# Seven products for eight in half of the blocks of the second MLP's down projection

## The chip, the core and the metric

The kernel runs on one core of a Trainium2 chip. The metric is device time in microseconds. Five engines work beside each other, each through a queue of its own in order: TensorE (PE; its weight loads are listed as PEld), VectorE (DVE), ScalarE (ACT), GpSimd (POOL) and SyncE (SP), which issues most of the DMAs. They are ordered among each other by semaphores that the program writes out by hand: a waiting instruction holds up everything behind it on its engine.

## What is computed

Two layers over 256 frames of 2048 channels, in float32. Each layer ends in an MLP, and the second layer's is what matters here:

```python
D_MODEL = 2048; SEQ = 256; D_FF = 4 * D_MODEL
...
        h = rmsnorm(x, ffn_norm[layer])
        x = x + jnp.square(jax.nn.relu(h @ w_up[layer])) @ w_down[layer]
```

`w_up` is 2048 x 8192 and `w_down` 8192 x 2048. The hidden layer is worked through in four quarters of 2048.

## The kernel before

**Precision by splitting.** Every weight is split into a high part (ScalarE's rounding copy, `Wh`, L1160) and the rest (VectorE's subtraction, `Wl`, L1585); the left operand likewise, into the halves of `A1` and `A2`. A product is high x high + high x low + low x high, three matmuls in the down projection.

**Weights.** They come in units of 512 KB, 1024 columns per partition, through four buffers `raw`, `Wh`, `Wl`. SyncE loads a unit into a raw buffer when VectorE has done the low split of the unit that was in it (`lo_split`). ScalarE splits it when it has landed and TensorE has finished the unit that held the buffer before (`unit_done`); VectorE follows (`hi_split`), TensorE waits for `lo_split`.

**Up projection.** Per quarter eight blocks of 256 hidden channels (`pair`, L710), four units each. The block's result lies in two PSUM banks of `ps`; blocks alternate between two pairs of banks. When it is done, ScalarE copies the crossed terms out (L1165), VectorE adds them to the rest (L1659, counted in `pair_read`), multiplies by the norm (L1918), squares the positive part (L1920, `hid_ready`), and ScalarE (L1539) and VectorE (L1923) split the result into `A2`. On both engines these steps stand behind the four splits of the next block's units.

**Down projection.** Per quarter four column blocks of 512 (`token_block`, L671). A unit is 256 hidden rows x 512 columns: for both halves of the 256 frames and both of its hidden chunks of 128, three matmuls with 512 columns, 12 in all (L681 to L683). A column block's two banks are accumulated over 8 units; then VectorE adds them to `xin` (`block_read`, L1680) while the next block accumulates in the other two banks. The bank set `px` is not used in this stage, and GpSimd has no work in the second MLP.

**Loops.** SyncE, ScalarE and VectorE run the quarters as loops (`load_mlp`, `double_pairs`, `downs`); TensorE's program is written out.

Of the kernel before, what the change touches and what calls it, by code (L numbers as in the profile page):

```python
# [32 lines left out]
P = 128  # L33
# [103 lines left out]
def trunk_kernel(nc, x, mix_norm_e, w_in_e, conv_w, conv_b, lru_wa, lru_ba, lru_wx, lru_bx, lru_lambda,  # L137
# [4 lines left out]
    with ctx:  # L142
# [46 lines left out]
        with ExitStack() as o:  # L189
            lt = sb("lt", [P, LC, L], on=o)  # L190
# [162 lines left out]
        zeroed = sem("zeroed")  # L353
        block = ctx.enter_context(nc.Block())
# [117 lines left out]
        def block_banks(g0, b):  # L472

            return 2 * ((g0 + b) % 2)

# [19 lines left out]
        def _(sp):  # L495
# [128 lines left out]
            load_mlp(P_MLP1, 1, blocks=True)  # L624
# [3 lines left out]
            for b in range(3):  # L628
                sp.wait_ge(pair_read, g + 2 * (b + 1))
                sp.dma_start(frames[:, :, bass.ts(b, 512)], xin[:, :, bass.ts(b, 512)]).then_inc(out_stored, 16)  # L630
# [7 lines left out]
        def _(pe):  # L638
# [32 lines left out]
            def token_block(g, d, at, freed, by_halves=False, beside=None):  # L671

                pe.wait_ge(pair_read, freed)

                def products(u, h):
                    for c in range(2):
                        k = 2 * u + c
                        high = A2[:, k, h * P:h * P + P]
                        low = A2[:, k, L + h * P:L + h * P + P]
                        to = ps[:, d + h, :]  # L680
# [18 lines left out]
            def opening(form, b, A):  # L699
# [4 lines left out]
                for c, low in order:  # L704
                    if low:
                        mm(ps[:, b, 0:L], Wl[:, 0, c, 0:P], A[:, c, 0:L], start=False, stop=False)
                    else:
                        mm(ps[:, b, :], Wh[:, 0, c, 0:P], A[:, c, :], start=(c == 0), stop=False)

            def pair(g, d, A, ready=None, base=0, per_unit=0, turn=0, beside=None, freed=None, form=None):  # L710


                b = 2 * d
# [4 lines left out]
                for s in range(NU):  # L718
# [3 lines left out]
                    if form and s == 0:  # L722
                        opening(form, b, A)
                    for t in range(1 if form and s == 0 else 0, 2):
                        for c in range(UK):
# [3 lines left out]
                            mm(ps[:, b + t, :], Wh[:, s, c, cols], A[:, k, :], start=(n == 0), stop=False)  # L729
                            last = mm(ps[:, b + t, 0:L], Wl[:, s, c, cols], A[:, k, 0:L], start=False, stop=(n == KC - 1))  # L730
# [378 lines left out]
            def token_mlp(g0, a1_at, a1_unit, a2_at, norm):  # L1109
# [13 lines left out]

                for q in range(QTR):
                    for j in range(8):
                        g = q * 16 + j + g0
                        freed = g - 1
                        if j == 0:
                            freed = g - 2 if q else g0 - 4
                        if q == 0 and j == 1:  # L1130
                            freed = g0 - 4
                        pair(g, g % 2, A1, a1_ready, a1_at, a1_unit, freed=freed,
                             beside=last_block if q == 0 and j == 0 else None,
                             form=entry_form(q, j))
                    for b in range(4):
                        g = q * 16 + (g0 + 8 + 2 * b)
                        token_block(g, block_banks(g0, b), q * 8 + a2_at, g - 2 if b else g - 1,
                                    by_halves=q == QTR - 1 and b == 3)
# [5 lines left out]
        def _(act):  # L1144
# [387 lines left out]
            def token_mlp(g0):  # L1532

                def up(j, d, q=0):
                    first = isinstance(q, int) and q == 0 and isinstance(j, int) and j == 0
                    pair(q * 16 + j + g0, (g0 + d) % 2, beside=last_operand if first else None)
                    hid.wait(act)
                    c = (g0 + d) % 2
                    hi.inc(fn(A2[:, bass.ds(j * 2, 2), 0:L], cross[:, c], ACT.Copy))  # L1539

# [11 lines left out]
                def downs(q, n=8):  # L1552
                    for j in range(n):
                        for s in range(NU):
                            split(q * 16 + (g0 + 9 + j), s)

                double_pairs(act, 8, up, (hi, 2), (hid, 2), first=2)
                downs(0)
                with trips(act, QTR - 2, (hi, 8), (hid, 8)) as q:
                    double_pairs(act, 8, lambda j, d: up(j, d, q + 1), (hi, 2), (hid, 2))  # L1560
                    downs(q + 1)
                double_pairs(act, 8, lambda j, d: up(j, d, QTR - 1), (hi, 2), (hid, 2))
                downs(QTR - 1, 7)

# [4 lines left out]
        def _(dve):  # L1569
# [374 lines left out]
            def token_mlp(g0):  # L1944
# [10 lines left out]
                def token_up(j, d, q=0):  # L1955
                    first = isinstance(q, int) and q == 0 and isinstance(j, int) and j == 0
                    up(g0, j, d, q, False, after=q * 8 + j + (CROSSED1 + 1),
                       beside=last_operand if first else None)

                double_pairs(dve, 8, token_up, (hi, 2), (seq, 2), first=2)  # L1960
                downs(g0, 0)
                with trips(dve, QTR - 2, (hi, 8), (seq, 8)) as q:
                    double_pairs(dve, 8, lambda j, d: token_up(j, d, q + 1), (hi, 2), (seq, 2))
                    downs(g0, q + 1)
                double_pairs(dve, 8, lambda j, d: token_up(j, d, QTR - 1), (hi, 2), (seq, 2))
                downs(g0, QTR - 1, halved=2)
# [458 lines left out]


# [27 lines left out]
```

## Time and profile before

| | |
|---|---|
| median of 3 runs | 1984.74 us (1984.61 to 1985.82) |
| profiled execution, span from first to last instruction | 1982.2 us |
| TensorE busy | 1953.0 us, 99% |
| VectorE, ScalarE, GpSimd busy | 1251.1, 916.4, 648.3 us |
| mean granted clock of TensorE | 0.995 of full speed |

The profile is one execution, recorded instruction by instruction. It gives for each instruction its start, its duration and the idle time before it with what ended that. The second MLP runs from about 1276 us to the end. In the records a matmul of 512 columns lasts 0.39 us, but matmuls are pipelined and their ends are modelled: the distance between starts is what one costs. Durations of GpSimd instructions include time in which they stand.

### The profile page before, as it was taken

The page shows a single profiled execution, that of the slowest core. Times are in us where ns is not written, and L with a number is a line of the kernel's source. Part 1 is how long each engine was busy: PE and PEld are TensorE (multiplying, and loading weights), DVE is VectorE, ACT ScalarE, POOL GpSimd, SP SyncE. Part 2 cuts the span into 40 slices and gives each one's busy share as a digit, 9 for nine tenths or more (in the row PEclk, how much of TensorE's full clock was granted, in tenths as well). Part 3 has the DMA queues.
Part 4 walks back from the last instruction along what each step waited for, and adds up shares of the span by engine and source line. Part 5 has one row for each costly group of instructions (what it writes and reads, how often), then busy time and mean ns, then how long its engine had stood idle before and what let it go on. Part 6 is the DMA issues. An engine that isn't in the chain of part 4 may idle for free.

```text
span 1982.2 us, 31585 instructions
## 1 busy us (share of the span) xinstructions
PE 1953.0 (99%) x11578; PEld 1651.1 (83%) x11578; DVE 1251.1 (63%) x1378; ACT 916.4 (46%) x1222; POOL 648.3 (33%) x858
## 2 busy tenths in 40 slices
PE   8999999999999999999998999999999999999999
PEld 7888788888888888888877888888888888888887
DVE  6885768755765576566559655576556556655654
ACT  6467654443443444344453544544344434434443
POOL 3592439778687778440019300000000000000000
PEclk9999999999999999999998999999999999999999
DMA  7644576666666666686788666655665666566654
GB/s 226 181 134 144 175 197 194 204 231 210 206 210 224 211 204 232 206 268 193 251 281 303 183 183 199 184 181 192 193 192 188 195 195 188 190 196 183 197 194 162
DMA packets 285582, 400.19 MB, mean 202 GB/s; under 512 B 23328, under 2 KB 185264, under 8 KB 283408
## 3 DMA queue, kind: packets, MB, share of 16 engines
q1 hardware_dynamic: 278032, 371.77, 59.7%
q0 software_dynamic: 5216, 24.52, 4.0%
q8 instruction: 93, 1.52, 0.3%
q10 hardware_dynamic: 2208, 2.11, 0.3%
q14 instruction: 33, 0.27, 0.0%
HBM read 371.87 MB, written 25.17 MB: 200 GB/s over the span
## 4 chain that ended last, share of the span: by engine, by line
PE 92%; DVE 2%; ACT 2%; DMA 1%; POOL 1%; issue 1%; SPq 0%; ACTq 0%; DVEq 0%; POOLq 0%
PE ps L729 27%; PE ps L730 13%; PE ps L681 12%; PE ps L683 12%; PE ps L682 12%; PE px L1059 1%; PE px L1061 1%; PE px L1060 1%; PE ps L1059 1%; PE ps L1060 1%; PE ps L1061 1%; PE px L945 1%; DMA raw<-in_w_up_dram 1%; PE ps L666 1%; DVE Wl L1585 1%
## 5 line engine op out<-in xcount | busy, mean ns | idle before, releaser
L1585 DVE TENSOR_TENSOR Wl<-raw,Wh 128x1024 fp32r<-128x1024 f32 x660 | 843.6, 1288 | 616.9 <-ACT Wh L1160 614.6
L1160 ACT ACTIVATE Wh<-raw 128x1024 fp32r<-128x1024 f32 x660 | 691.8, 1059 | 750.7 <-PE ps L683 377.3
L729 PE MATMUL ps<-A,Wh 128*128 128x512 f32 x2364 | 830.1, 396 | 2.7 <-DVE A L1672 2.3
L730 PE MATMUL ps<-A,Wl 128*128 128x256 f32 x2364 | 657.6, 278 | 0.0
L729 PEld LDWEIGHTS ps<-A,Wh 128*128 128x128 f32 x2364 | 443.3, 188 | 108.7 <-issue 5.1
L730 PEld LDWEIGHTS ps<-A,Wl 128*128 128x128 f32 x2364 | 444.7, 188 | 0.3
L681 PE MATMUL ps<-Wh,A 128*128 128x512 f32 x1024 | 399.8, 390 | 0.0
L683 PE MATMUL ps<-Wh,A 128*128 128x512 f32 x1024 | 398.5, 389 | 0.0
L682 PE MATMUL ps<-Wl,A 128*128 128x512 f32 x1024 | 398.4, 389 | 0.0
L683 PEld LDWEIGHTS ps<-Wh,A 128*128 128x128 f32 x1024 | 192.2, 188 | 40.3
L681 PEld LDWEIGHTS ps<-Wh,A 128*128 128x128 f32 x1024 | 192.2, 188 | 39.9
L682 PEld LDWEIGHTS ps<-Wl,A 128*128 128x128 f32 x1024 | 192.2, 188 | 39.5
L1923 DVE TENSOR_TENSOR A<-cross,A 128x512 f32 (+1 forms) x64 | 47.1, 736 | 57.6 <-ACT A L1539 32.5
L1411 ACT ACTIVATE A<-cross 128x512 fp32r<-128x512 f32 (+1 forms) x32 | 20.3, 634 | 106.4 <-DVE cross L1920 106.4
L1539 ACT ACTIVATE A<-cross 128x512 f32 (+1 forms) x32 | 20.3, 634 | 95.8 <-DVE cross L1920 95.8
L1659 DVE TENSOR_TENSOR cross<-ps,cross 128x512 f32<-128x512 f32 x75 | 51.2, 683 | 7.7 <-ACT cross L1165 7.6
L2375 POOL DMA_DIRECT2D us<-s_u x8 | 7.2, 897 | 139.8 <-DMA s_u<-uc 139.8
L1059 PE MATMUL ps<-Wh,A 128*128 128x512 f32 x128 | 51.1, 399 | 1.0 <-DVE Wl L1585 1.0
L1680 DVE TENSOR_TENSOR xin<-ps,xin 128x512 f32<-128x512 f32 x68 | 43.8, 682 | 11.2 <-PE ps L683 11.2
L2325 POOL TENSOR_TENSOR t<-cti,lamp 128x256 f32<-128x256 f32 x16 | 21.6, 1352 | 89.0 <-ACT cti L1365 89.0
L1920 DVE SCALAR_TENSOR_TENSOR cross<-cross 128x512 f32<-128x512 f32 x64 | 48.6, 760 | 2.2
L1059 PE MATMUL px<-Wh,A 128*128 128x512 f32 x128 | 50.0, 390 | 0.0
(376 smaller groups left out, 2035.5 us busy)
## 6 DMA issues: line engine op xcount, KB each, us to landing
raw<-in_w_up_dram SPq DMA_DIRECT2D x256, 512.0 KB, 3.9
raw<-in_w_down_dram SPq DMA_DIRECT2D x256, 512.0 KB, 3.9
raw<-in_w_glu_dram SPq DMA_DIRECT2D x64, 512.0 KB, 4.4
raw<-in_w_in_e_dram SPq DMA_DIRECT2D x52, 512.0 KB, 3.9
raw<-in_w_out_e_dram SPq DMA_DIRECT2D x32, 512.0 KB, 3.8
s_params<-stg POOLq DMA_DIRECT2D x16, 1024.0 KB, 6.1
slot<-s_params SPq DMA_DIRECT2D x12, 768.0 KB, 7.3
slot<-s_params SPq DMA_DIRECT2D x12, 256.0 KB, 7.5
```

The lines of the kernel that those rows point to most:

```text
L681: mm(to, high, wide(Wh, u % NU)[:, c], start=(k == 0), stop=False)
L682: mm(to, high, wide(Wl, u % NU)[:, c], start=False, stop=False)
L683: last = mm(to, low, wide(Wh, u % NU)[:, c], start=False, stop=(k == KC - 1))
L729: mm(ps[:, b + t, :], Wh[:, s, c, cols], A[:, k, :], start=(n == 0), stop=False)
L730: last = mm(ps[:, b + t, 0:L], Wl[:, s, c, cols], A[:, k, 0:L], start=False, stop=(n == KC - 1))
L1059: mm(to, high, wide(Wh, u % NU)[:, c], start=(k == 0), stop=False)
L1160: fn(Wh[:, s], raw[:, s], ACT.Copy).then_inc(hi_split, 1)
L1585: tt(Wl[:, s], raw[:, s], Wh[:, s].bitcast(F32), ALU.subtract).then_inc(lo_split, 1)
L1659: tt(cross[:, d] if dest is None else dest, banks[:, :, 0:L], cross[:, d], ALU.add).then_inc(pair_read, 1)
L1680: tt(to, banks[:, h, :], to, ALU.add).then_inc(pair_read, 1)
L1920: stt(cross[:, c], cross[:, c], 0.0, cross[:, c], ALU.max, ALU.mult).then_inc(hid_ready, 1)
L1923: tt(A2[:, k, L:2 * L], cross[:, c], A2[:, k, 0:L].bitcast(F32), ALU.subtract).then_inc(a2_ready, 1)
```

## The change

In the down projection of the second MLP, 256 hidden rows x 1024 output columns now form a group (two units). Even groups of each pass are multiplied as two-by-two block products (frames x hidden chunks, hidden chunks x column blocks of 512) with seven products after Strassen and Winograd, odd groups plainly. The last column half of the last quarter stays plain (`is_summed`). A pass is one quarter and one column half.

For a summed group four sums of `A2`'s blocks are needed (`sa`, on GpSimd, once per quarter, made beside the up projection and split into `sah` and `sal`), and four differences of weight blocks (`wt`, on GpSimd, from `raw`, and split into `Th` and `Tl`). `wt`, `Th` and `Tl` exist once. A raw buffer of a summed group is free only when GpSimd has made the last difference from it (`wt_second`). Products 1, 5, 6 and 7 are accumulated over a pass in the four banks of `px`, products 2, 3 and 4 and the plain groups in the four banks of `ps`. At the end of a pass ScalarE copies `px` to `pq`, VectorE adds `ps` to `xin`, and GpSimd adds the sums of `pq` to it. Blocks of the up projection are spread over `ps` and `px`. ScalarE's, VectorE's and SyncE's loops of this stage are written out.

The core of the diff; TensorE first:

```diff
+                def summed_group(q, p, m):
...
+                    def p1():
+                        pe.wait_ge(lo_split, u + 1)
+                        three(px[:, 0, :], *a(0, 0), s0, 0, first, last)
+                    def p2():
+                        if first:
+                            pe.wait_ge(pair_read, freed + (1 if p else 0))
+                        three(ps[:, 0, :], *a(1, 0), s0, 1, first, False).then_inc(unit_done, 1)
+                    def p3():
+                        if first:
+                            pe.wait_ge(pair_read, freed + (2 if p else 0))
+                        pe.wait_ge(lo_split, u + 2)
+                        three(ps[:, 1, :], *summed_a(3), s1, 1, first, False).then_inc(unit_done, 1)
+                    def p5_p7():
+                        pe.wait_ge(wt_lo, 2 * n + 1)
+                        three(px[:, 1, :], *summed_a(0), 0, 0, first, last, Th, Tl)
+                        three(px[:, 3, :], *summed_a(2), 1, 0, first, last, Th, Tl)
+                    def p6():
+                        pe.wait_ge(wt_lo, 2 * n + 2)
+                        three(px[:, 2, :], *summed_a(1), 2, 0, first, last, Th, Tl)
+                    def p4():
...
+                        three(ps[:, 2, :], *a(1, 1), 3, 0, first, False, Th, Tl).then_inc(wt_done, 1)
...
+                        order = (p1, p5_p7, p6, p2, p3, p4)
+                    else:
+                        order = (p1, p2, p3, p5_p7, p6, p4)
```

SyncE's loads of the down projection, and GpSimd's sums:

```diff
+                            sp.wait_ge(lo_split, u - NU + 1)
+                            if n < 4 and p == 1 and n < 2:
+                                sp.wait_ge(wt_second, summed_no(q, 0, 6) + 1)
+                            if n >= 4 and not plain and is_summed(q, p, n // 2 - 2):
+                                sp.wait_ge(wt_second, summed_no(q, p, n // 2 - 2) + 1)
...
+            def summed_rows(q, j):
+                pool.wait_ge(hid_ready, 8 * QTR + q * 8 + j + 1)
...
+                tt(sa[:, 2], a11, a21, ALU.subtract)
+                link(tt(sa[:, 0], a21, a22, ALU.add))
+                link(tt(sa[:, 1], sa[:, 0], a11, ALU.subtract))
+                tt(sa[:, 3], a12, sa[:, 1], ALU.subtract).then_inc(sa_sum, 1)
+            def weight_sums(q, p, m):
+                for k in range(2):
+                    pool.wait_ge(landed[u % NU + k], (u // NU + 1) * 16)
+                if n:
+                    pool.wait_ge(wt_lo, 2 * n)
...
+                tt(wt[:, 0:2], wide(raw, u % NU + 1), both, ALU.subtract).then_inc(wt_first, 1)
+                pool.wait_ge(wt_first, n + 1)
+                link(tt(wt[:, 2], wide(raw, u % NU + 1)[:, 1], wt[:, 0], ALU.subtract))
+                tt(wt[:, 3], wide(raw, u % NU)[:, 1], wt[:, 2], ALU.subtract).then_inc(wt_second, 1)
+            def first_outputs(q, p):
+                pool.wait_ge(px_out, 4 * (2 * q + p) + 4)
+                link(tt(pq[:, 2], pq[:, 2], pq[:, 0], ALU.add))
+                link(tt(pq[:, 3], pq[:, 3], pq[:, 2], ALU.add))
+                pool.wait_ge(pair_read, P_MLP1 + q * 16 + 8 + 4 * p + 4)
+                tt(columns(p, 0), columns(p, 0), pq[:, 0:4:3], ALU.add).then_inc(x_summed, 1)
...
+                for m in range(0, 8, 2):
+                    weight_sums(q, 0, m)
+                if q < QTR - 1:
+                    weight_sums(q, 1, 0)
+                    first_outputs(q, 0)
+                    weight_sums(q, 1, 2)
+                    second_outputs(q, 0)
+                    weight_sums(q, 1, 4)
+                    weight_sums(q, 1, 6)
```

ScalarE's order (VectorE's follows it, with `outputs_read` of a pass behind the first unit of the next pass's second group):

```diff
+                def summed_weights(q, p, m):
+                    if n:
+                        act.wait_ge(wt_done, n)
+                    act.wait_ge(wt_first, n + 1)
+                    fn(Th[:, 0:2], wt[:, 0:2], ACT.Copy).then_inc(wt_hi, 1)
+                    act.wait_ge(wt_second, n + 1)
+                    fn(Th[:, 2:4], wt[:, 2:4], ACT.Copy).then_inc(wt_hi, 1)
+                def group(q, p, m, read=None):
+                    unit(u)
+                    if read:
+                        products_out(*read)
+                    if is_summed(q, p, m):
+                        second_column(q, p, m)
+                        summed_weights(q, p, m)
+                    else:
+                        unit(u + 1)
+                def up(q, j):
+                    if j < 7:
...
+                    else:
+                        group(q, 0, 0)
+                        summed_rows(q, 6)
+                        group(q, 0, 1)
+                    act.wait_ge(unit_done, (g + 1) * NU)
...
+                    cross_terms(j % 2, up_banks(q, j))
+                    hid.wait(act)
```

## Rows read from the trace of the kernel before

**Rows 1.** The page's first part: busy us (share of the span) xinstructions of each engine.
```profile
PE 1953.0 (99%) x11578; PEld 1651.1 (83%) x11578; DVE 1251.1 (63%) x1378; ACT 916.4 (46%) x1222; POOL 648.3 (33%) x858
```

**Rows 2.** The list of waits, from 1300 to 1960 us: total us, times, longest.
```profile
DVE Wl L1585 <- ACT Wh L1160: 235.1, 180, 1.6
ACT Wh L1160 <- PE ps L683: 183.7, 112, 1.7
ACT Wh L1160 <- PE ps L730: 101.3, 66, 1.8
...
```

**Rows 3.** Busy us in one quarter's down projection: us, PE, PEld, DVE, ACT, POOL, granted clock, DMA.
```profile
1364.00:1451.30 87.30, 87.30 (x388) 72.30 (x387) 45.44 (x43) 34.88 (x34) 0.00 (x0) 1.00 0.62 197
```

**Rows 4.** The timeline of TensorE in a down projection: start us, us, engine, line.
```profile
1560.54 0.39 PE L681 MATMUL ps<-Wh,A 128*128 128x512 f32 x1
...
1576.86 0.39 PE L681 MATMUL ps<-Wh,A 128*128 128x512 f32 x1
```

**Rows 5.** The timelines of ScalarE, VectorE and SyncE's queue in down projections.
```profile
1559.38 1.06 ACT L1160 ACTIVATE Wh<-raw 128x1024 fp32r<-128x1024 f32 x1 [1.66 <-PE ps L683]
...
1560.48 1.23 DVE L1585 TENSOR_TENSOR Wl<-raw,Wh 128x1024 fp32r<-128x1024 f32 x1 [1.49 <-ACT Wh L1160]
...
1561.95 0.37 SPq L510 DMA_DIRECT2D raw<-in_w_down_dram  x1
...
1453.86 1.28 DVE L1680 TENSOR_TENSOR xin<-ps,xin 128x512 f32<-128x512 f32 x2
```

**Rows 6.** The timelines of SyncE's queue and ScalarE after the S5 stage: a burst of loads.
```profile
1111.01 1.45 SPq L592 DMA_DIRECT2D raw<-in_w_glu_dram  x3
...
1114.95 1.06 ACT L1160 ACTIVATE Wh<-raw 128x1024 fp32r<-128x1024 f32 x1 [0.22 <-DMA raw<-in_w_glu_dram]
1116.37 1.06 ACT L1160 ACTIVATE Wh<-raw 128x1024 fp32r<-128x1024 f32 x1 [0.36 <-DMA raw<-in_w_glu_dram]
```

**Rows 7.** GpSimd by line and by form: busy us, mean ns (or min/median/max).
```profile
L2218 POOL TENSOR_TENSOR la<-lr x2: 1894/1894/1895, 199.8 to 201.6; 128x1024 f32<-128x1024 f32 x2
L2399 POOL TENSOR_TENSOR pp<-pp x16: 1179/1188/2106, 1043.9 to 1102.2; 128x512 f32<-128x512 f32 x16
L2235 POOL TENSOR_TENSOR stg<-t 128x128 f32<-128x128 f32 x16 | 8.7, 542 | 1.3
```

**Rows 8.** The timelines of GpSimd and VectorE where both work on SBUF operands.
```profile
1102.22 2.11 POOL L2399 TENSOR_TENSOR pp<-pp 128x512 f32<-128x512 f32 x1 [1.50 <-DVE pp L2036]
1104.29 1.83 POOL L2405 TENSOR_TENSOR A<-yt,A 128x256 fp32r<-128x256 f32 x1
...
1103.18 2.23 DVE L1585 TENSOR_TENSOR Wl<-raw,Wh 128x1024 fp32r<-128x1024 f32 x1
1107.13 1.88 DVE L1585 TENSOR_TENSOR Wl<-raw,Wh 128x1024 fp32r<-128x1024 f32 x1
```

**Rows 9.** The same timelines where VectorE reads one operand from PSUM.
```profile
1081.90 0.85 POOL L2405 TENSOR_TENSOR A<-yt,A 128x256 fp32r<-128x256 f32 x1
1082.71 1.26 POOL L2393 TENSOR_TENSOR zb<-ab 128x512 f32<-128x512 f32 x1
...
1083.31 0.68 DVE L2021 TENSOR_TENSOR ab<-px,slot 128x512 f32<-128x512 f32 x1
```

**Rows 10.** The timelines of ScalarE and VectorE at the end of up blocks.
```profile
1357.92 0.64 ACT L1539 ACTIVATE A<-cross 128x512 f32 x1 [2.97 <-DVE cross L1920]
...
1364.50 1.06 ACT L1160 ACTIVATE Wh<-raw 128x1024 fp32r<-128x1024 f32 x1 [1.71 <-PE ps L730]
...
1369.02 0.64 ACT L1539 ACTIVATE A<-cross 128x512 f32 x1 [2.96 <-DVE cross L1920]
...
1368.18 0.69 DVE L1920 SCALAR_TENSOR_TENSOR cross<-cross 128x512 f32<-128x512 f32 x1
```

**Rows 11.** Busy us in windows of the S5 stage, columns as in rows 3.
```profile
1034.00:1036.00 2.00, 0.29 (x6) 0.32 (x8) 1.56 (x7) 1.50 (x3) 0.76 (x1) 0.50 0.76 267
...
1064.00:1070.00 6.00, 3.97 (x130) 3.70 (x124) 5.97 (x10) 2.24 (x5) 5.54 (x6) 1.00 1.08 384
```

More of the change, by code:

```diff
@@ L1562, in token_mlp, with unit, second_column @@
[L1562 to L1563 removed]
+                def unit(u):
+                    split(u // NU, u % NU)
+                def second_column(q, p, m):
+                    u = down_unit(q, p, m) + 1
+                    act.wait_ge(landed[u % NU], (u // NU + 1) * 16)
+                    act.wait_ge(unit_done, u - NU + 1)
+                    fn(wide(Wh, u % NU)[:, 1], wide(raw, u % NU)[:, 1], ACT.Copy).then_inc(hi_split, 1)
@@ new lines, in token_mlp @@
+                for q in range(QTR):
+                    for j in range(8):
+                        up(q, j)
+                    for m in range(2, 8):
+                        group(q, 0, m)
+                    if q < QTR - 1:
+                        for m in range(8):
+                            group(q, 1, m, read=(q, 0) if m == 0 else None)
+                        g = (q + 1) * 16 + g0
+                        split(g, 0)
+                        products_out(q, 1)
+                        for s in range(1, NU):
+                            split(g, s)
@@ L1565, in _ @@
+                g = (QTR - 1) * 16 + g0 + 12
+                split(g, 0)
+                products_out(QTR - 1, 0)
+                for s in range(1, NU):
+                    split(g, s)
+                for n in range(1, 4):
+                    for s in range(NU):
+                        split(g + n, s)
             token_mlp(P_MLP1)
@@ new lines, in plain_group, with up @@
+                def plain_group(q, p, m, read=None):
+                    u = down_unit(q, p, m)
+                    unit(u)
+                    if read:
+                        outputs_read(*read)
+                    unit(u + 1)
+                def up(q, j):
+                    g = q * 16 + j + g0
+                    if j < 7:
+                        for s in range(NU):
+                            split(g + 1, s)
+                            if q == 0 and j == 0:
+                                last_operand(s)
+                            if j % 2 and s == 1:
+                                summed_rows(q, j - 1)
+                    else:
+                        summed_group(q, 0, 0)
+                        summed_rows(q, 6)
+                        plain_group(q, 0, 1)
+                    c = j % 2
+                    evict(g, c, banks=up_banks(q, j), after=q * 8 + j + (CROSSED1 + 1))
+                    link(tt(cross[:, c], cross[:, c], rs2, ALU.mult))
+                    stt(cross[:, c], cross[:, c], 0.0, cross[:, c], ALU.max, ALU.mult).then_inc(hid_ready, 1)
+                    hi.wait(dve)
+                    tt(A2[:, 2 * j:2 * j + 2, L:2 * L], cross[:, c], A2[:, 2 * j:2 * j + 2, 0:L].bitcast(F32), ALU.subtract)\
+                        .then_inc(a2_ready, 1)
@@ new lines, in token_mlp @@
+                for q in range(QTR):
+                    for j in range(8):
+                        up(q, j)
+                    for p in range(2):
+                        if q == QTR - 1 and p == 1:
+                            break
+                        for m in range(2 if p == 0 else 0, 8):
+                            if is_summed(q, p, m):
+                                summed_group(q, p, m)
+                            else:
+                                plain_group(q, p, m, read=(q, 0) if p == 1 and m == 1 else None)
+                    if q < QTR - 1:
+                        g = (q + 1) * 16 + g0
+                        for s in range(3):
+                            split(g, s)
+                        outputs_read(q, 1)
+                        split(g, 3)
```

265 lines of the change are left out of this document (218 added, 47 removed).

## The prediction

> **What bounds the kernel now.** I read the page's busy times first: TensorE is busy for 99% of the span [rows 1]. A modelled busy time proves little, so the list of waits over most of the second MLP comes next. It has five lines, the three longest stand in [rows 2]: VectorE waits for ScalarE and ScalarE for TensorE, and in none of the five is TensorE the one that waits. The down projection of one quarter of the hidden layer lasts 87.3 us, TensorE has no gap in it, GpSimd does nothing at all, and VectorE and ScalarE are busy for 45 and 35 us [rows 3]. Inside it a matmul of 512 columns starts every 16.32/72 = 0.2267 us (first and last of 73 starts in [rows 4]). So TensorE's number of matmuls sets this stage, and the other engines have room: a unit of weights (512 KB, 12 matmuls) comes every 2.72 us and costs ScalarE 1.06 and VectorE 1.23 [rows 5].
>
> **What the change removes.** Call 256 hidden rows by 1024 output columns a group. It is 24 matmuls now and 21 where the seven products are used, and that is the even four of eight groups in seven of the eight passes (quarter by column half): 28 x 3 = 84 matmuls, 84 x 0.2267 = 19.0 us. A pair of groups, one of each kind, asks TensorE for 45 x 0.2267 = 10.2 us, where it takes 10.9 now. 19.0 us is the most that it can give.
>
> **What it adds beside TensorE.** Per pair: ScalarE 3.5 units of split, which become 5.5 (5.8 us); VectorE the same (some 6.4 us at 1.15 each back to back); GpSimd one difference of 1024 columns and two of 512. GpSimd's prices: 1.89 for 1024 with one tensor read twice, 1.19 for 512 [rows 7]; I take 2.1 and 1.2, 4.5 a group, 4.2 to 4.9 as ends. The Trainium skill (GPSIMD Engine Reference, section 3.1) gives 4497 ns for 2048 fp32 columns; halved that is an estimate of 2.25 for 1024, a little dearer than the row, and by it each group below would be 0.15 later and the sum some 3 us larger. All these totals fit into 10.2. The extra work in the up projection (four GpSimd operations on 128 columns, one 512-column split on ScalarE and VectorE per two up blocks) lies in a stage of 22.2 us per two blocks [rows 10] where each of them has room; I cost it at nothing there (if that cover were gone: 0.7 us a time, 16 times). What decides is order and buffers.
>
> **GpSimd and VectorE don't run side by side.** A GpSimd operation of 512 columns that takes 1.19 alone took 2.11 when a VectorE split was running, one of 256 columns 1.83 instead of 0.85, and a split 1.88 to 2.23 instead of 1.23 [rows 5, 7, 8, 9]; in that stretch the two engines take turns, one instruction each. VectorE instructions with one operand in PSUM are untouched, 0.68 beside a GpSimd operation [rows 9]. All of VectorE's splits read two SBUF operands, the new ones too.
>
> **The new loop.** The two raw buffers of a summed group may now be reloaded only when GpSimd has read them for the last time (`wt_second`), and GpSimd may begin the next only when both have landed. In us from one `wt_second`: SyncE issues 0.24 later [rows 5]. Loads issued back to back land in turn: the first split of such a burst starts 3.94 after the first issue, the second 5.36 [rows 6]. So GpSimd has both at 5.6. VectorE's split of the first (landed 4.1, ScalarE to 5.2) holds the port until 6.4; first difference until 8.5; VectorE's half split 0.6; second difference 9.1 to 10.3; VectorE's split of the first differences 1.15; third difference to 12.7. If GpSimd gets its turn first each time it is 11.7; with no wait at all 5.6 + 4.2 = 9.8. I take 12.2. TensorE wants a pair every 10.2: wherever the loop has no head start, a pair costs 12.2, more than the 10.9 of now. On SyncE only the plain group's loads are queued behind the new wait, and they are due half a pair later.
>
> **Start of a down projection.** All eight PSUM banks are accumulators now, so the second product needs the last up block read. Count from that block's end. GpSimd's row sums of up block 7 wait for its squares, ready 3.68 + 0.69 = 4.4 after its end [rows 10], that is at 4.4 - 11.1 = -6.7; four operations at 0.54 [rows 7] and one turn of VectorE bring it to -4.2; three differences with turns end at about 1.9 (0 with no waits, 2.6 with all). ScalarE stands in front of exactly this: behind the second half of the differences are queued the row split, two units and only then the crossed terms of the last up block; on VectorE it is four splits (1.15, 0.69, 1.15, 1.15) and the read. That puts the read about 6.0 after `wt_second`, at 7.9, where TensorE has run out at 2.7 (12 matmuls). Stall 5.2, ends 3.3 and 5.9. Now this costs nothing: two bank pairs alternate. (ScalarE's four copies out of the other accumulators, 0.6 each, lie beside a plain group's 5.4 us and hold nobody up.)
>
> **The sum, per quarter.** Pair 1: 10.2 + 5.2 = 15.4. Pair 2 has its loads early: 10.2. Pair 3: its reload also waits for the splits of pair 2, which ScalarE reaches only after the last up block's squares (about 15), so differences come at 15.3 + 12.2 = 27.5 where TensorE wants them by 26.6: 11.1. Pair 4 goes by the loop: 12.2. First half 48.9 against 43.5 now: +5.4.
> Second half, pair 5: differences 12.2 after those of pair 4, 3.3 late for the order used there; then VectorE must split a unit (1.15), with one GpSimd turn (1.2), before it reads the first output bank (0.64 [rows 5]), so the second product starts at 8.2 instead of 2.7: 15.7. Pair 6: GpSimd's queue holds the output sums ahead of its differences: they wait for the fourth read (10.2), add 1024 columns (2.1 and a turn, 13.4), then 4.5 + 0.2 + 2.5 of turns, 20.6, that is 3.9 late; the second output sums (two of 1024 columns) then hold VectorE's splits up by some 2.4: 16.5. Pair 7: 11.0. Pair 8, by the loop less what was ahead: 11.9. Together 55.1 against 43.5: +11.6. The last quarter has no such second half, its plain columns cost what they cost now.
> Sum: 4 x 5.4 + 3 x 11.6 = 56.4 us. The profiled execution's span of 1982.2 would become 2038.6; the median of the runs, 1984.74, lies 2.5 above that span, and I carry the difference over: 2041, rounded to 2040. With the low ends (start 3.3, loop 11.7) the first half is +3.5 and the second +9.3: +42; with the high ends (5.9 and 12.7) +6.8 and +13.2: +67. This case's own range is 2027 to 2052.
>
> **The rivals.**
> The loop is shorter than 10.2, and the change gains. Price: 19.0 less four starts of about 2 = 11 us, 1974. It decides at GpSimd waits of less than 0.4 per group on top of 9.8: turns fall into VectorE's gaps, or the second load lands sooner because the first is already done. Against it: VectorE's split of the same landing comes 0.2 before GpSimd's first difference by construction, and the two engines took strict turns in [rows 8]. Chance 0.11.
> The turns cost half of what I count (loop 11.0, start 3.5). First half +1.6, second half +5.6 (starts 13.5, 14.0, 10.6, 11.0): 4 x 1.6 + 3 x 5.6 = 23, 2008. For it: VectorE is idle for nearly half of this stage now [rows 3]. Chance 0.20.
> TensorE's clock falls in the stalls. The granted clock was at half, 1.2 GHz, in a stretch where TensorE had done 0.29 us of work in 2 us; at about two thirds busy it kept 2.4 GHz [rows 11]. My start leaves TensorE nearly idle from 2.7 to 7.9, pairs 5 and 6 are about 60% busy. If it falls at each start and twice in each second half, at about 3 us a time: 4 x 3 + 3 x 6 = 30 on top, 2071. Chance 0.12.
> Gain and stalls cancel, within 4 us: 0.05.
>
> **How the numbers follow.** My forecast has 0.52. A difference of 0.2%, 4 us, is about what a measurement of this kernel tells from none. Faster: the first rival, 0.11. Same: 0.05. Slower: 0.52 + 0.20 + 0.12 = 0.84. The range takes in the forecast, most of the second rival and half of the third: 1997 to 2071.
>
> **What the changed profile would show.** Right: TensorE waits in the second MLP's down stretches, for VectorE's splits of the differences and, at the starts, for the crossed-terms read; quarters of more than 100 us where 87.3 stood, the last quarter least hurt; GpSimd's first difference of a group starting 5 to 7 us after the previous `wt_second`, with durations of twice the price alone. Wrong: down stretches of 82 to 85 us without waits of TensorE (the first rival); GpSimd durations all at the price alone (the turns don't happen); a granted clock under 1 there (the third).

## The result and the profile after

The changed kernel takes 2054.74 us (median of 4 runs, 2052.02 to 2057.49) where the kernel before takes 1985.28 beside it: ratio 1.0349, interval 1.0334 to 1.0364. It is slower by 69.5 us; 2040 was forecast. Executions that fell in a slow state of the chip are left out of every figure here and below. The span of the profiled execution grew from 1982.2 to 2050.2. Of its page, the busy times and the chain that ended last (shares by engine) come first.

```profile
PE 1968.0 (96%) x11494; PEld 1646.8 (80%) x11494; DVE 1420.3 (69%) x1450; ACT 975.1 (48%) x1322; POOL 973.2 (47%) x1041
...
PE 70%; DVE 11%; POOL 10%; DMA 4%; ACT 3%; issue 2%; SPq 0%; POOLq 0%; ACTq 0%; DVEq 0%
```

TensorE has the 84 matmuls fewer of [rows 1], yet its busy time rose from 1953.0 to 1968.0: many of its matmuls were slower. GpSimd's busy time went up by half, and it and VectorE now hold a fifth of the chain. TensorE, which waited for nobody in [rows 2], has these lines in the list of waits from 1270 to 2040 us (total, times, longest):

```profile
PE px L1198 <- DVE Tl L2206: 33.6, 22, 2.9
PE ps L1198 <- DVE cross L1893: 9.4, 4, 2.5
PE ps L1198 <- DVE xin L2221: 5.6, 3, 1.9
PE ps L1198 <- DVE Wl L1819: 4.0, 4, 1.7
PE ps L798 <- DVE A L1906: 1.0, 1, 1.0
```

The first four, 52.6 us, lie in the seven down passes that were changed: waits for the split differences (`Tl`), for the read of the last up block at the starts (`cross`), for the output read (`xin`), for a weight split (`Wl`). Busy times of the two halves of the first quarter's down projection and of ten us behind its start (columns as in rows 3):

```profile
1363.30:1414.20 50.90, 44.27 (x182) 35.15 (x181) 38.75 (x29) 26.28 (x32) 26.86 (x13) 0.93 0.50 166
1414.20:1470.00 55.80, 48.02 (x181) 37.09 (x180) 45.20 (x28) 25.32 (x29) 39.08 (x18) 0.88 0.49 158
...
1370.00:1380.00 10.00, 7.63 (x24) 6.09 (x25) 9.23 (x8) 3.80 (x6) 5.60 (x3) 0.66 0.42 147
```

Where one quarter took 87.3 us at clock 1.00 [rows 3] it takes 106.7, and the granted clock is under 1 in both halves. TensorE's timeline at this start shows how both losses follow each other:

```profile
1363.31 0.39 PE L1198 MATMUL px<-Wh,A 128*128 128x512 f32 x1
...
1363.77 0.40 PE L1200 MATMUL px<-Wh,A 128*128 128x512 f32 x1
1365.40 0.50 PE L1198 MATMUL px<-Th,sah 128*128 128x512 f32 x1 [1.24 <-DVE Tl L2206]
1365.74 0.40 PE L1199 MATMUL px<-Tl,sah 128*128 128x512 f32 x1
...
1368.90 0.50 PE L1198 MATMUL px<-Th,sah 128*128 128x512 f32 x1 [1.84 <-DVE Tl L2206]
...
1372.37 0.80 PE L1198 MATMUL ps<-Wh,A 128*128 128x512 f32 x1 [2.51 <-DVE cross L1893]
...
1375.10 0.63 PE L1198 MATMUL ps<-Th,A 128*128 128x512 f32 x1
1375.52 0.63 PE L1199 MATMUL ps<-Tl,A 128*128 128x512 f32 x1
...
1377.23 0.41 PE L1200 MATMUL ps<-Wh,A 128*128 128x512 f32 x1
1377.47 0.39 PE L1198 MATMUL ps<-Wh,A 128*128 128x512 f32 x1
```

Three waits, 5.59 us in all. In the third the granted clock falls, and it stays at half until 1377.25 (busy times, columns as in rows 3):

```profile
1370.42:1377.25 6.83, 4.88 (x12) 3.83 (x13) 6.15 (x5) 0.63 (x3) 5.07 (x3) 0.50 0.55 189
```

So after the third wait a matmul starts every 0.43 us instead of 0.23: TensorE goes on at 1.2 GHz until 1377.2. Each pair of groups is measured between the starts of the first matmuls of two pairs. What it takes over the 10.2 of its 45 matmuls at 2.4 GHz is split into the listed waits, what its matmuls lose while the granted clock is at half, and an edge (us, means over four quarters in the first half, three in the second). The edge is lost at full clock, almost all of it around waits: a wait is counted only from the modelled end of the matmul before it, 0.40 after that one's start (1363.77 above), and the first matmul behind it takes 0.34 to the next start (1365.40 to 1365.74).

| pair | forecast | measured | of it waits | of it half clock | of it edges |
|---|---|---|---|---|---|
| 1 | 15.4 | 18.4 | 5.3 | 2.3 | 0.6 |
| 2 | 10.2 | 10.2 | 0 | 0 | 0 |
| 3 | 11.1 | 10.2 | 0 | 0 | 0 |
| 4 | 12.2 | 11.5 | 1.0 | 0 | 0.4 |
| 5 | 15.7 | 18.2 | 4.9 | 2.5 | 0.7 |
| 6 | 16.5 | 16.4 | 3.7 | 2.0 | 0.5 |
| 7 | 11.0 | 10.3 | 0 | 0 | 0.1 |
| 8 | 11.9 | 11.1 | 0.6 | 0 | 0.3 |

The clock is at half in nine stretches of these passes: in all four first pairs, all three fifth and two of the three sixth. Waits 52.6, half clock 22.6 and edges 8.8, less the 19.0 saved, make 65.0 of the 68.0 us by which the span grew. The up stretches, where the output sums of the second column half now run, hold 4.3 more (89.2 to 90.7 us, before 88.7); ahead of the first down projection 1.0 is gained.

GpSimd's loop, in its timeline of the same half (start, us, line, then the wait before it):

```profile
1397.73 3.19 POOL L2776 TENSOR_TENSOR wt<-raw 128x1024 f32<-128x1024 f32 x1 [5.33 <-DMA raw<-in_w_down_dram]
1400.99 1.63 POOL L2778 TENSOR_TENSOR wt<-raw,wt 128x512 f32<-128x512 f32 x1
1402.70 2.16 POOL L2779 TENSOR_TENSOR wt<-raw,wt 128x512 f32<-128x512 f32 x1
1410.20 3.19 POOL L2776 TENSOR_TENSOR wt<-raw 128x1024 f32<-128x1024 f32 x1 [5.34 <-DMA raw<-in_w_down_dram]
```

From one group's first difference to the next it is 12.47 us, 5.3 of it a wait for the loads; TensorE wants one every 10.2. By line and form, over the whole second MLP (busy, mean ns):

```profile
L1819 DVE TENSOR_TENSOR Wl<-raw,Wh 128x1024 fp32r<-128x1024 f32 x226 | 330.3, 1489 | 76.6 <-ACT Wh L1322 73.6
L2776 POOL TENSOR_TENSOR wt<-raw 128x1024 f32<-128x1024 f32 x28 | 85.8, 3064 | 104.2 <-DMA raw<-in_w_down_dram 104.2
...
L2197 DVE TENSOR_TENSOR Wl<-raw,Wh 128x512 fp32r<-128x512 f32 x28 | 53.7, 1916 | 3.7 <-ACT Wh L1716 3.7
```

A split of 1.23 [rows 5] takes 1.49 in the mean, and one of half the columns, which takes 0.68 at its shortest, 1.92: 19 of its 28 took 1.57 to 2.89.

### The profile page after: what moved, and what is told of

Its sections match the earlier page's. It is cut to its first block, busy times and chain, and to the rows that moved or that the text cites. A ratio compares the mean times of both kernels' runs of the same rounds, so it can differ in the third digit from the quotient of the medians.

```text
span 2050.2 us, 30441 instructions
## 1 busy us (share of the span) xinstructions
PE 1968.0 (96%) x11494; PEld 1646.8 (80%) x11494; DVE 1420.3 (69%) x1450; ACT 975.1 (48%) x1322; POOL 973.2 (47%) x1041
## 4 chain that ended last, share of the span: by engine, by line
PE 70%; DVE 11%; POOL 10%; DMA 4%; ACT 3%; issue 2%; SPq 0%; POOLq 0%; ACTq 0%; DVEq 0%
PE ps L798 20%; PE ps L799 10%; PE ps L751 6%; PE ps L753 6%; PE ps L752 6%; DVE Wl L1819 6%; POOL wt L2776 3%; DMA raw<-in_w_down_dram 3%; PE px L798 2%; POOL wt L2779 2%; POOL wt L2778 2%; PE px L1128 1%; PE px L1129 1%; PE px L1130 1%; PE ps L1128 1%
## 5 line engine op out<-in xcount | busy, mean ns | idle before, releaser
L798 PE MATMUL ps<-A,Wh 128*128 128x512 f32 x1992 | 703.8, 398 | 2.8 <-DVE A L1906 1.9
L799 PE MATMUL ps<-A,Wl 128*128 128x256 f32 x1992 | 555.6, 279 | 0.0
L751 PE MATMUL ps<-Wh,A 128*128 128x512 f32 x544 | 213.0, 392 | 0.0
L753 PE MATMUL ps<-Wh,A 128*128 128x512 f32 x544 | 211.8, 389 | 0.0
L752 PE MATMUL ps<-Wl,A 128*128 128x512 f32 x544 | 211.7, 389 | 0.0
L2776 POOL TENSOR_TENSOR wt<-raw 128x1024 f32<-128x1024 f32 x28 | 85.8, 3064 | 104.2 <-DMA raw<-in_w_down_dram 104.2
L798 PE MATMUL px<-A,Wh 128*128 128x512 f32 x372 | 130.1, 395 | 0.0
L2206 DVE TENSOR_TENSOR Tl<-wt,Th 128x1024 fp32r<-128x1024 f32 x56 | 78.1, 1404 | 72.2 <-ACT Th L1726 45.4
L1198 PE MATMUL ps<-Wh,A 128*128 128x512 f32 x252 | 104.4, 414 | 19.0 <-DVE cross L1893 9.4
L751 PEld LDWEIGHTS ps<-Wh,A 128*128 128x128 f32 x544 | 102.1, 188 | 21.5
L753 PEld LDWEIGHTS ps<-Wh,A 128*128 128x128 f32 x544 | 102.1, 188 | 21.4
L752 PEld LDWEIGHTS ps<-Wl,A 128*128 128x128 f32 x544 | 102.2, 188 | 20.8
L799 PE MATMUL px<-A,Wl 128*128 128x256 f32 x372 | 103.5, 278 | 0.0
L1199 PE MATMUL ps<-Wl,A 128*128 128x512 f32 x252 | 102.3, 406 | 0.0
L1200 PE MATMUL ps<-Wh,A 128*128 128x512 f32 x252 | 101.5, 403 | 0.0
L798 PEld LDWEIGHTS px<-A,Wh 128*128 128x128 f32 x372 | 69.8, 188 | 16.6
L1198 PEld LDWEIGHTS ps<-Wh,A 128*128 128x128 f32 x252 | 49.9, 198 | 34.9 <-DVE cross L1893 11.4
```

What stands on the lines that cost most here:

```text
L798: mm(banks[:, t, :], Wh[:, s, c, cols], A[:, k, :], start=(n == 0), stop=False)
L799: last = mm(banks[:, t, 0:L], Wl[:, s, c, cols], A[:, k, 0:L], start=False, stop=(n == KC - 1))
L1198: mm(to, high, wh, start=first, stop=False)
L1199: mm(to, high, wl, start=False, stop=False)
L1200: return mm(to, low, wh, start=False, stop=last)
L2206: tt(Tl[:, k], wt[:, k], Th[:, k].bitcast(F32), ALU.subtract).then_inc(wt_lo, 1)
```

## The experiments

The theory was that of the forecast: GpSimd's differences take turns with VectorE's splits, and with the reload they make a loop longer than TensorE's 10.2 us; the starts wait for the read of the last up block. Against it stood that the port is innocent and the loop's length, the clock or the products themselves cost the time. Each figure is set against the kernel before on the same chip (1983.9 to 1986.2 us).

**Without the turns.** In two kernels GpSimd's differences are mostly left out (the products then use zeros or stale columns). In the first they run on 32 of 512 columns, in the second they are fills of the same length, which only write:

```diff
-tt(wt[:, 0:2], wide(raw, u % NU + 1), both, ALU.subtract).then_inc(wt_first, 1)
+link(nc.gpsimd.memset(wt[:, 0:2], 0.0))
+link(nc.gpsimd.memset(wt[:, 0:2], 0.0))
+nc.gpsimd.memset(wt[:, 0:1], 0.0).then_inc(wt_first, 1)
...
```

> GpSimd makes the weight differences on 32 of 512 columns only (the rest of the tile is zero, so a part of the down projection's products is left out); all waits, loads and splits stay. My theory: the loop from one last difference to the next (measured 12.5 us) shrinks to 5.6 of loading plus about 1.5 of GpSimd, 7 us, under TensorE's 10.2; TensorE's waits for the splits of the differences go in pairs 4, 6 and 8, the start keeps about 2 of its 5.3 us. Total 1965 to 1990 us where the change takes 2054.7. Rival: the queues of ScalarE and VectorE, which do as much as in the change, set the stage: above 2030.

> The weight differences are left out and replaced by fills of the same tile that read nothing, seven instructions that keep GpSimd busy for a like time (4.5 to 5.5 us per group), so that GpSimd stands at the same place in the loop but needs no read port. My theory: the fills take their time alone in every group (least and most within 10%), VectorE's splits beside them fall back to 1.2 us, the loop is 5.6 plus the fills, 10.2 to 11.2 us, and the total 1995 to 2030. Rival, GpSimd's length alone and not the turns with VectorE: the loop stays above 12 and the total above 2045.

> The same kernel as e2_no_port (the weight differences are left out and replaced by fills that read nothing), for an undisturbed profile of it. My theory: fills of one length in every group, VectorE's splits in the down projections at 1.2 us beside them, the loop 10.2 to 11.2 us, total 1995 to 2030. Rival, GpSimd's length alone and not the turns: loop above 12, total above 2045.

Short differences: 1986.37, a single execution without a trace that can be used. Fills: 2010.51 in a single execution, then 2007.66 (ratio 1.012, 1.010 to 1.014). GpSimd is at work for 4.9 us a group, about as long as the differences would take alone, and its timeline shows the loop:

```profile
1391.75 0.96 POOL L2776 MEMSET wt<- 128x1024 f32 x1 [5.44 <-DMA raw<-in_w_down_dram]
...
1401.95 0.95 POOL L2776 MEMSET wt<- 128x1024 f32 x1 [5.30 <-DMA raw<-in_w_down_dram]
```

The same wait for the loads, but the loop is 10.20, TensorE's own pace, and pairs 2 to 4 take 10.2 each. The 46 splits of 1024 columns that met a fill and no other GpSimd operation took 1.22 us in the mean, like the 169 that met nothing. So of the 69.5 us, 45.7 (69.5 - 23.8) come from turns. The one execution with short differences lies another 24 us below the fills on the same chip (2010.51), which suggests, and no more, that GpSimd's length without turns costs something too. The Trainium skill (SBUF — State Buffer, Who interferes with whom) says that a VectorE instruction with two SBUF inputs contends with a GpSimd instruction that reads SBUF and not with one that only writes it. These two kernels agree.

What is left in the kernel of the fills is the starts (16.6 us, with the 2.5 for the last up block still there) and pairs 5 and 6 (11.5 and 14.8).

**The reload.** GpSimd makes its differences from a tensor that stays in place (the differences are then of the wrong data), and SyncE no longer waits for `wt_second`:

```diff
-if n >= 4 and not plain and is_summed(q, p, n // 2 - 2):
-    sp.wait_ge(wt_second, summed_no(q, p, n // 2 - 2) + 1)
...
-tt(wt[:, 0:2], wide(raw, u % NU + 1), both, ALU.subtract).then_inc(wt_first, 1)
...
+one, other = A1[:, 0:2, :].bitcast(F32), A1[:, 2:4, :].bitcast(F32)
+tt(wt[:, 0:2], one, other, ALU.subtract).then_inc(wt_first, 1)
...
```

> GpSimd takes its differences from another tile of the same kind (the result is left without the right weights' differences), so that the raw buffers needn't wait for it: SyncE reloads them when VectorE has split them, as before. All instructions and lengths stay. My theory: the 5.6 us of loading leave the loop; what is left is the next start 2.4 after the last difference (both splits of it) and 6.8 of GpSimd, 9.2, under 10.2; so pairs 3, 4, 7 and 8 are 10.2 long, pair 5 loses its waits for the differences (3 us), pair 6 keeps only what the output sums cost; total 2015 to 2032. Rival, the length of GpSimd's work with its turns is what counts and the reload is hidden: no change, 2050 or more.

2052.78, no change, as the rival said. But its trace doesn't bear the rival out. GpSimd in the first quarter (timeline):

```profile
1371.68 2.59 POOL L2771 TENSOR_TENSOR wt<-A 128x1024 f32<-128x1024 f32 x1 [2.58 <-DVE Tl L2200]
...
1400.73 3.14 POOL L2771 TENSOR_TENSOR wt<-A 128x1024 f32<-128x1024 f32 x1 [5.49 <-DMA raw<-in_w_down_dram]
...
1410.38 3.16 POOL L2771 TENSOR_TENSOR wt<-A 128x1024 f32<-128x1024 f32 x1 [2.58 <-DVE Tl L2200]
```

Before the fourth group the wait for the load is there as before, 5.49: SyncE also waits for VectorE's splits of the same buffers (`lo_split`), and with the turns these end as late as GpSimd's last difference (1395.78 and 1395.23 here). Where the load was early (the second and the fifth group) GpSimd starts 2.58 after its last difference, and pair 5 falls by 3.0 us in the mean. The gain is lost at the starts: GpSimd's second group now comes 3.0 us sooner after the first, beside the two splits that stand before the read of the last up block. VectorE's timelines, here:

```profile
1371.97 5.58 DVE L1813 TENSOR_TENSOR Wl<-raw,Wh 128x1024 fp32r<-128x1024 f32 x2
```

and in the changed kernel:

```profile
1369.36 2.35 DVE L1819 TENSOR_TENSOR Wl<-raw,Wh 128x1024 fp32r<-128x1024 f32 x2
```

TensorE waits 5.74 for that read instead of 2.51, and pair 1 takes 21.9 in the mean instead of 18.4: 4 x 3.5 = 14 lost, 3 x 3.0 and four fourth pairs at 10.2 instead of 11.5 gained. What the reload alone costs stays open, since this edit didn't take it away.

**The clock.** Dummy matmuls, thrown away, fill TensorE's waits in the first groups:

```diff
+def filler(bank, count):
+    for _ in range(count):
+        mm(bank, a(0, 0)[0], wide(Wh, s0)[:, 0], start=True, stop=True)
...
-order = (p1, p5_p7, p6, p2, p3, p4)
+order = (p1, filled_p5_p7, filled_p6, filled_p2, p3, p4)
```

> TensorE multiplies into a bank that is free at that moment while it would wait in the first group of a pass: 7, 8 and, in first halves, 10 products that nobody reads (75 more than the work needs in each quarter but the last). Theory of the clock: the granted clock stays at full in pair 1 and, but for its last wait, in pair 5; pair 1 goes from 18.4 to about 15.8, pair 5 from 18.2 to 15.6 to 17; total 2030 to 2042 although TensorE does more. Rival, the long matmuls there come from contention or from the weight loads: pairs 1 and 5 as long as before or longer, 2050 to 2065.

2058.21 (1.0363, 1.0333 to 1.0393): the rival's time, but the theory's clock. Busy times of pair 1:

```profile
1365.90:1382.50 16.60, 16.37 (x71) 12.94 (x71) 12.90 (x11) 7.82 (x11) 8.69 (x5) 1.00 0.40 127
```

The clock stays at 1.00, pair 1 falls from 18.4 to 16.5 and pair 5 from 18.2 to 16.7, where the rival had them as long as before: the slow matmuls were the clock, not contention or weight loads. But pairs 3 and 4 rise to 11.7 and 13.2 (means), and the first half lasts 51.6 us instead of 50.4 (the second 55.8 instead of 56.0). GpSimd's last difference of the second, third and fourth group ends 14.53, 28.85 and 41.88 us after the start here, 14.48, 29.09 and 41.55 in the changed kernel (the fourth 41.9 and 41.0 in the mean of the quarters): this chain doesn't come sooner when TensorE's clock stays up, and it sets where the half ends. In the first halves, half clock is a loss that TensorE would otherwise spend waiting.

**The start.** GpSimd makes the first group's differences before the row sums of the last up block pair:

```diff
-for j in range(0, 8, 2):
+for j in range(0, 6, 2):
     summed_rows(q, j)
-for m in range(0, 8, 2):
+weight_sums(q, 0, 0)
+summed_rows(q, 6)
+for m in range(2, 8, 2):
     weight_sums(q, 0, m)
```

> One change of order in GpSimd's queue: the differences of a quarter's first group stand before the row sums of the last up block but one, not behind them. My theory: they are done before the up projection ends, ScalarE reaches the last up block's crossed terms some 5 us sooner, TensorE's waits at the start of a down projection fall from 5.3 to under 1.5 us, and its clock doesn't fall there (3 us each): 4 x 6.5 = 26 us, about 2028 (2020 to 2036). Rival, the start is set by the eight accumulators alone: no change at the start, 2050 or more.

2044.66 (1.0295, 1.0265 to 1.0325): 58.6 us above the kernel before instead of 69.5, 10.9 less, where 26 had been expected. The differences begin 8.1 us before the down projection instead of 3.3, but the row sums come late and meet VectorE in their turn:

```profile
1363.19 0.91 POOL L2762 TENSOR_TENSOR sa<-cross 128x128 f32<-128x128 f32 x1
1364.06 1.45 POOL L2763 TENSOR_TENSOR sa<-cross 128x128 f32<-128x128 f32 x1
```

The four take 4.6 us instead of 3.2; ScalarE's copy of the sums waits for them, and the read stands behind that copy. Pair 1 falls to 16.1 in the mean, and one of the four (17.9) gains next to nothing.

**The differences on VectorE.** GpSimd keeps the row sums and the output sums; VectorE subtracts between its splits. In a second kernel ScalarE and VectorE also read the last up block before the row split and the next group:

```diff
-summed_rows(q, 6)
-group(q, 0, 1)
...
 cross_terms(j % 2, up_banks(q, j))
+if j == 7:
+    summed_rows(q, 6)
+    group(q, 0, 1)
...
```

> VectorE makes the four weight differences, in turn with its splits; GpSimd keeps the row sums and the output sums. My theory: without turns the loop is 5.6 + 4.1 = 9.7, under 10.2, and VectorE has 8.8 us of work per pair of 10.2; first halves 41 to 44 us; in second halves GpSimd's output sums (9.6 us of reads) take turns with a VectorE that has only 3 us to spare, 42 to 48 us. Total 1970 to 2000. Rival, VectorE has no room for 2.4 us more per pair: pairs above 10.9 and the total above 2010.

> e7, and ScalarE and VectorE read the last up block right after the first group's splits, before the row split and the next group's units. My theory of the start: the second product finds its bank read at about 2 us, the waits at the start (2 to 3 us in e7) are gone and with them a lower clock: 8 to 16 us less than e7, 1958 to 1988. Rival, the start doesn't depend on this order: the same as e7.

2006.65 (1.0113, 1.0096 to 1.0130) and 1997.83 (1.0069, 1.0053 to 1.0086). With the differences in one queue with the splits 46.7 of the 69.5 us are gone, much as with the fills, though VectorE does more; pairs 2 to 4 take 10.2 (with the early read 11.2, 10.2 and 10.2). The early read takes pair 1 from 14.4 to 10.7 and is worth 8.8 us, near the low end of what was expected. Both totals lie above what was expected: pairs 5 and 6 stay at 14.2 to 15.2 and 13.4 to 15.0. GpSimd's output sums are what still meets VectorE there (timelines of GpSimd, then of VectorE, in the first of these kernels):

```profile
1419.21 3.24 POOL L2789 TENSOR_TENSOR xin<-xin,pq 128x1024 f32<-128x1024 f32 x1 [6.57 <-DVE xin L2221]
1422.53 3.24 POOL L2794 TENSOR_TENSOR pq<-pq 128x1024 f32<-128x1024 f32 x1
```

```profile
1420.12 3.42 DVE L2232 TENSOR_TENSOR wt<-raw 128x1024 f32<-128x1024 f32 x1
1423.46 3.40 DVE L1819 TENSOR_TENSOR Wl<-raw,Wh 128x1024 fp32r<-128x1024 f32 x1
```

**What the products alone give.** From the last kernel, the output sums on 32 of 512 columns, and then the differences too (most of both is left out; every matmul, split, read and wait stays):

```diff
-link(tt(pq[:, 2], pq[:, 2], pq[:, 0], ALU.add))
+link(tt(pq[:, 2, 0:32], pq[:, 2, 0:32], pq[:, 0, 0:32], ALU.add))
...
-tt(wt[:, 0:2], wide(raw, u % NU + 1), both, ALU.subtract).then_inc(wt_first, 1)
...
+tt(wt[:, 0:2, 0:32], wide(raw, u % NU + 1)[:, :, 0:32], both[:, :, 0:32], ALU.subtract).then_inc(wt_first, 1)
...
```

> The kernel at 1997.83 with every output sum of GpSimd on 32 of its 512 columns (most of the sums are left out, order and waits are kept). Theory (GpSimd's output sums hold VectorE up): pairs 5 and 6 at 10.2 to 11.2, 1971 to 1980, and no more than 4 us below the kernel that moves these sums into the up stretch. Rival (VectorE is full by itself): above 1988.

> As the one before, with VectorE's differences on 32 of 512 columns as well (most of the differences and of the output sums are left out, order, waits and every matmul are kept). What is left is the products alone, with their splits and reads. Theory (84 matmuls of 0.2267 us are the gain, and all else of the loss is GpSimd's and VectorE's extra work): 1984 less 19.0 and some 1 to 5 us for the starts, 1964 to 1971. Rival (the products themselves cost: their splits, their eight accumulators, their order): above 1975.

1973.57 (0.9938, 0.9922 to 0.9955) and 1967.80 (0.9906, 0.9890 to 0.9923), both in the range of their theories. The first theory's other condition failed: 1973.57 lies 18 us, not at most 4, below the kernel that moves these sums into the up stretch, shown next. In the second every pair takes 10.19 to 10.26, and TensorE has no wait in the down passes; the busy times of the first quarter's pairs in it:

```profile
1367.40:1449.00 81.60, 81.60 (x362) 67.54 (x361) 60.12 (x77) 50.52 (x58) 4.26 (x7) 1.00 0.65 209
```

So the 84 matmuls are worth 18.4 us by the medians, 19.0 by the count. The output sums cost 26.6 us (14.0 + 12.6, against each one's own before), VectorE's differences 5.8.

**The output sums elsewhere.** The differences stay on VectorE, the read stays early, and the first column half's output sums are put off, with a second set of buffers, into the next up stretch, where the other half's are made. In a second kernel the row sums of the first up block are taken ahead of the other half's output sums:

```diff
-pool.wait_ge(px_out, 4 * (2 * q + p) + 4)
+pool.wait_ge(px_out, 4 * (2 * q + p) + (4 if p or q == QTR - 1 else 8))
...
 summed_rows(q, j)
+if q and j == 0:
+    first_outputs(q - 1, 1)
+    second_outputs(q - 1, 1)
```

> VectorE makes the differences and reads the last up block early, as in the kernel at 1997.83; in addition the output sums of the first column half wait until the second column half has been copied out too, so that GpSimd does both sets in the next up stretch and nothing at all in the down stretches. In the kernel at 1997.83 pairs 5 and 6 take 14.9 and 14.1 us (means of three quarters), the others 10.2 to 11.2. Theory (these two pairs are long because GpSimd's five output sums, 1.3 to 3.25 us each, take turns with VectorE's splits): pairs 5 and 6 fall to 10.2 to 11.2, that is about 7 us in each of three quarters, the up stretches grow by at most 1 us each: 1974 to 1983. Rival (VectorE is simply full, some 9.4 of 10.2 us a pair with the differences on it, and the four output reads of 0.68 push it over): pairs 5 and 6 stay above 13, 1990 or more.

> The kernel at 1991.71 (differences on VectorE, last up block read early, output sums in the up stretch) with one thing moved in GpSimd's queue: the row sums of the first up block of a quarter come before the output sums of the second column half instead of after both halves' sums. In the trace of that kernel the down stretches hold 10.2 to 11.2 us a pair, and the three up stretches lasted 95.8 us against 89.15: ScalarE waited 3.97 us for the row sums, TensorE then 3.76 us, the rest is half clock behind that. Theory (only the queue order costs this): the three waits go, up stretches of 89 to 91 us, 1971 to 1980, below the kernel before. Rival (the turns of GpSimd's two sets of sums with VectorE's splits hold the up blocks up wherever they stand): up stretches stay above 93 us, 1984 or more.

1991.71 (1.0032, 1.0020 to 1.0043) and 1990.59 (1.0030, 1.0020 to 1.0041). In the down passes the theory held: pairs 5 and 6 at 10.5 to 10.9 and 10.2. But the first total missed its range of 1974 to 1983: the up stretches, 88.7 us before, went to 95.4 and then 93.9 us (means), where the theory allowed 1 us more, and the second kernel gave its rival right. Busy times of an up stretch, first in the kernel before, then in the second of these:

```profile
1451.30:1540.00 88.70, 88.70 (x514) 77.53 (x512) 58.53 (x62) 40.29 (x46) 0.00 (x0) 1.00 0.60 186
```

```profile
1447.40:1541.90 94.50, 91.00 (x515) 78.40 (x514) 76.65 (x71) 41.64 (x50) 34.60 (x26) 1.00 0.55 173
```

VectorE is now busy for 77 of the 94 us. Its timeline there:

```profile
1470.73 2.89 DVE L2218 TENSOR_TENSOR sal<-sa,sah 128x512 fp32r<-128x512 f32 x1
1473.54 6.75 DVE L1826 TENSOR_TENSOR Wl<-raw,Wh 128x1024 fp32r<-128x1024 f32 x2
```

Two splits of 1.23 take 6.75 beside the output sums, the read of the block's result behind them comes late, and TensorE waits 3.5 us in three pieces. Moving the sums moved their price. These two are the fastest versions that compute everything, and neither is faster than the kernel before.

## Why the prediction was right or wrong

The direction and the range were right, the number in part by luck: it had TensorE's lost time 14.0 us too long and its slow clock, 22.6 us, at nothing, and the two errors cancel in good part. The time came out 14.7 us above the forecast, 2.7 above the forecast's own range, and about halfway to the third rival (2071, chance 0.12).

**The gain** of 19.0 us: right, 18.4 measured with everything else out of the way.

**The turns**: right. They were the ground of the forecast, and fills instead of differences took 45.7 of 69.5 us away. The prices: 2.36 alone for the 1024 columns (shortest in the trace) where 2.1 was taken, 1.29 for 512 where 1.2 was; with turns 3.19, 1.63 and 2.16. The Trainium skill's 4497 ns for 2048 columns (GPSIMD Engine Reference, section 3.1), halved an estimate of 2.25, was the nearer one of the two. The second rival, turns at half price and 2008, fell: the half splits took 1.92 in the mean where 0.68 is the shortest.

**The loop** of 12.2: right, 12.46 and 12.47 to the fourth and fifth group, and its landing at 5.6 was 5.33. To the third group it was 14.6. `wt_second` is the release that comes last here, as told (VectorE's half split of the fourth group ends 3.4 us before it); without it, VectorE's own splits under turns hold the buffers as long. The chain set the first half: differences of the third and fourth group forecast at 27.5 and 39.7 (27.5 + 12.2) after the start, measured 29.1 and 41.6. The first rival, a loop under 10.2, fell; with the fills alone the loop is 10.20.

**The start**: the chain was right to 1.3 us (last difference at 3.2 instead of 1.9 after the end of up, the last up block read at 9.0 instead of 7.9), the loss at full clock too (5.9, waits and edges, instead of 5.2), though in three pieces and not one, since the products of the differences come first. What was missing is the clock.

**The clock**: the step that failed. The forecast had it at nothing, with one stretch at half clock to go by, 0.29 us of work in two [rows 11], and gave the case 0.12. It fell in pairs 1, 5 and 6, nine times at 2.5 us, 22.6 us in all; the third rival's own count is ten times 3.

**The waits**: too long by 14.0 us. The forecast holds 56.4 + 19.0 = 75.4 us of lost time at full clock, the trace 61.4 (waits 52.6, edges 8.8). Pair 6 was put 6.3 over 10.2 and has 4.2 of it, pairs 3, 4, 7 and 8 together 5.4 and have 2.4. A pair that is lengthened by half clock gives the loop behind it a head start: in the first halves the filler shows this, in the second it is argued. So the two errors hang together: waits and clock can't be added as if they were independent. Forecast and result agree better by halves (48.9 against 50.4, 55.1 against 56.0) than by causes. What is left of the 14.7 us is 3 outside these passes, and 3 of runs and rounding (the profiled execution was the fastest of the four).

**The output sums** were in the forecast only as 3.9 late and 2.4 more in pair 6. In the kernel with VectorE's differences they cost 26.6 us, more than the products bring. How much of the changed kernel's own 69.5 they hold wasn't measured there; the prices depend on what else fills VectorE.

## What to carry to other kernels

Work that is moved to an idle engine isn't free when both engines read SBUF: in this kernel count each GpSimd operation that reads SBUF as a lengthening of the VectorE instruction with two SBUF operands that it meets, up to 2.2 us on a split of 1.23. Before TensorE's work is cut by an eighth, leave the added work out in an experiment of its own: it shows the whole gain (here 19 us), and each part put back has its price read off (26.6, 5.8, 8.8, 46.7 here). Don't add a slow clock in full on top of waits where another engine's chain sets the end.

## What the runs showed of the hardware

A GpSimd fill of 512 columns takes 0.53 us and doesn't lengthen a split, a difference of the same size takes 1.29 and does. Where both engines had work queued (the timelines of the first kernel with VectorE's differences), they alternated, one whole instruction each: 1024-column subtractions of 1.23 on VectorE started every 3.3 us beside GpSimd additions of 3.24, of a size that takes 2.4 at its shortest.

At the start of a down projection three waits of 1.24, 1.84 and 2.51 us, with 1.4 us of work or less between them, went with a fall of the granted clock from 2.4 to 1.2 GHz inside the third, and the half clock outlasted that wait by 4.9 us. With waits of 0.8, 0.7 and 2.5 (the kernel with the fills) the first pair still lost 1.6 us at half clock, with a single one of 2.4 (the first kernel with VectorE's differences) 1.6 in three of the four quarters and nothing in the fourth.
